# The recurrent stage of a two-block transformer kernel: unscaled sum transposed, projections scaled by a row on VectorE, low parts of the down-sized weights made by GpSimd

## What is computed

```python
h = _rmsnorm(x, g[1])                      # x * rsqrt(mean(x*x) + eps) * gain, by token
p = h @ w_in                               # 1024 -> 3*512 (convolution) + 1696 (recurrence)
gate_b, gate_c, h_in = jnp.split(p_conv, 3, axis=-1)
y_conv = gate_b * _short_conv(gate_c * h_in, conv_w)           # 3 taps over the tokens
p_rwkv = p_rwkv + (_shift(p_rwkv) - p_rwkv) * mu_shift         # mixed with the token before
r, k, v, dw, da, dg = jnp.split(p_rwkv, _RWKV_SPLITS, axis=-1)
# decay and iclr from dw and da, keys normalised by head, then for each token, 8 heads of 64:
#   S = S * w + (S a) b^T + v k^T ;  y = S r
# y normalised by head, plus a bonus term, times a gate
return jnp.concatenate([y_conv, y_rwkv], axis=-1) @ w_out
```

## Time and profile before

| | us |
|---|---|
| median of 3 runs | 1487.98 (1487.74 to 1488.11) |
| the profiled execution, its own time | 1488.31 |
| its span from first to last instruction | 1486.5 |
| TensorE busy in the span | 1471.3 (99%) |
| VectorE busy | 1005.7 (68%) |
| ScalarE busy | 853.0 (57%) |
| GpSimd busy | 507.2 (34%) |

### The profile page before, as it was taken

How to read it: one execution, slowest core, us unless ns; L and a number is a source line. 1 busy time by engine, 2 the same in 40 slices (tenths; PEclk the granted TensorE clock), 3 DMA queues, 4 the chain that set the end, 5 groups by cost and what they waited for, 6 DMA issues and landing times. The chain is left out here.

```text
span 1486.5 us, 25655 instructions
## 1 busy us (share of the span) xinstructions
PE 1471.3 (99%) x9545; PEld 1279.4 (86%) x9545; DVE 1005.7 (68%) x1304; ACT 853.0 (57%) x1316; POOL 507.2 (34%) x207
## 2 busy tenths in 40 slices
PE   9999999999999999999999999999999999999998
PEld 8888889888888888888988888888888887888886
DVE  6776567567777567765665776557765589877654
ACT  6555576445555565555675655555555678655544
POOL 2434400001444335444341444434344300144442
PEclk9999999999999999999999999999999999999999
DMA  7655542235565645555533565545655453265552
GB/s 260 226 206 197 184 142 86 89 115 184 198 199 186 208 157 186 207 191 192 184 115 114 187 206 190 193 156 191 209 195 186 170 202 110 100 213 186 206 184 87
DMA packets 48812, 259.99 MB, mean 175 GB/s; under 512 B 5584, under 2 KB 5968, under 8 KB 28144
## 3 DMA queue, kind: packets, MB, share of 16 engines
q1 hardware_dynamic: 29520, 190.49, 36.5%
q10 hardware_dynamic: 19152, 68.53, 14.0%
q0 software_dynamic: 80, 0.14, 0.0%
HBM read 258.08 MB, written 1.05 MB: 174 GB/s over the span
## 5 line engine op out<-in xcount | busy, mean ns | idle before, releaser
L379 POOL TENSOR_TENSOR dn_lo<-raw_dn,dn_hi 128x1024 fp32r<-128x1024 f32 x138 | 471.8, 3419 | 833.7 <-ACT dn_hi L362 824.8
L366 DVE TENSOR_TENSOR gu_lo<-raw_gu,gu_hi 128x2048 fp32r<-128x2048 f32 x161 | 369.4, 2294 | 182.7 <-ACT gu_hi L352 181.4
L612 PE MATMUL banks<-h_both,gu_hi 128*128 128x512 f32 x2016 | 478.2, 390 | 0.0
L612 PEld LDWEIGHTS banks<-h_both,gu_hi 128*128 128x128 f32 x2016 | 378.1, 188 | 78.4 <-ACT gu_hi L352 0.2
L352 ACT CAST gu_hi<-raw_gu 128x2048 fp32r<-128x2048 f32 x160 | 305.0, 1906 | 12.1 <-PE banks L386 12.0
L619 PEld LDWEIGHTS banks<-h_both,gu_lo 128*128 128x128 f32 x2016 | 258.5, 191 | 9.8
L619 PE MATMUL banks<-h_both,gu_lo 128*128 128x256 f32 x2016 | 261.6, 283 | 0.0
L386 PE MATMUL banks<-dn_hi,act_hi 128*128 128x512 f32 x528 | 207.2, 393 | 0.0
L386 PE MATMUL banks<-dn_lo,act_hi 128*128 128x512 f32 x528 | 207.2, 392 | 0.0
L386 PE MATMUL banks<-dn_hi,act_lo 128*128 128x512 f32 x528 | 205.6, 389 | 0.0
L559 DVE TENSOR_TENSOR silu<-silu,arena 128x256 f32<-128x256 f32 x126 | 179.1, 1421 | 4.3
(11 more groups left out here) (392 smaller groups left out, 1565.7 us busy)
## 6 DMA issues: line engine op xcount, KB each, us to landing
raw_gu<-units_gu SPq DMA_DIRECT2D x161, 1024.0 KB, 4.8
raw_dn<-units_dn ACTq DMA_DIRECT2D x130, 512.0 KB, 3.5
raw_dn<-units_dn SPq DMA_DIRECT2D x32, 512.0 KB, 3.5
...
```

Source lines behind the costliest of these rows:

```text
L366: nc.vector.tensor_tensor(gu_lo[:, p, :], raw_gu[:, p, :], gu_hi[:, p, :].bitcast(F32), ALU.subtract).then_inc(gu_lo_ready, 1)
L379: nc.gpsimd.tensor_tensor(dn_lo[:, p, 0:n], raw_dn[:, p, 0:n], dn_hi[:, p, 0:n].bitcast(F32), ALU.subtract).then_inc(dn_lo_ready, 1)
L612: ins = nc.tensor.matmul(banks[:, 2 * p + side, :], gu_hi[:, p, w], h_both[:, k, :, :].rearrange("p i t -> p (i t)"), start=k == 0, stop=F ...
```

## The change

It does three things in the even stage, and leaves the others alone:

- The start takes the feed-forward stages' way: `gained_pe` on TensorE, then squares and root on ScalarE behind `h_hi`, and a row of factors, which stands in `silu[:, 0, :]` (`even_row`). TensorE makes the row behind tile 2. The seven matmuls, the two scalings of `x` and the GpSimd steps for eps are gone.
- A new step `raw(i)` on VectorE multiplies each tile by the row as it reads it from PSUM: for mixed tiles into a buffer of four (`unmixed`), for tiles 14 to 25 right into their place. `evac(i)` and `mix(i)` then read that buffer in SBUF, and `evac` is gone for tiles 14 to 25. A tile's bank is free after `raw`.
- All twelve `dn_lo` of the stage are made by GpSimd (`lo_dn_pool`) and none by VectorE (`lo_dn`). GpSimd does them behind a memset that waits for both squares.

```diff
@@ -284,6 +284,7 @@
...
+        even_row = silu[:, 0, :]
...
@@ -478,21 +479,25 @@
...
+        def row_bank(s):
+
+            return 3 if stages[s] == "even" else 7
+
         def rstd_row_pe(pe, s):
...
-                ins = nc.tensor.matmul(banks[:, 7, t * P:(t + 1) * P], const("ones"), rstd_diag[:, t, :], start=True, stop=True)
+                ins = nc.tensor.matmul(banks[:, row_bank(s), t * P:(t + 1) * P], const("ones"), rstd_diag[:, t, :], start=True, stop=True)
...
-            nc.scalar.copy(rstd_row, banks[:, 7, 0:T]).then_inc(row_ready, 1)
+            nc.scalar.copy(even_row if stages[s] == "even" else rstd_row, banks[:, row_bank(s), 0:T]).then_inc(row_ready, 1)
...
-            return sum(k == "ffn" for k in stages[:s])
+            return sum(k in ("ffn", "even") for k in stages[:s])
...
@@ -876,30 +881,32 @@
...
-            dve = [("scaled", t, c) for t in range(2) for c in range(2)] + ["omu", "omka"] + mix(0, 5) + ["one_row", "key_ss"] + mix(5, 8) + ["kkn", "b", "at", "bt"]
-            dve += ["kh", "mt0", "mt1"] + mix(8, 9) + ["ab0", "ab", "kt"] + mix(9, 10)
+            raw = lambda *places: [("raw", i) for i in places]
...
+            dve += ["rb"] + raw(15, 16) + ["bv", "bv_b"] + raw(17) + ["uw"] + raw(18) + ["s1"] + conv(0) + raw(19)
+            dve += [("q", 0), ("q", 1)] + state(1) + raw(20) + [("y", 1)]
+            dve += conv(1) + state(2) + raw(21) + [("y", 2)] + conv(2) + raw(22) + [("y", 3)] + conv(3) + raw(23) + ["centred"]
+            dve += raw(24, 25) + [("y_conv", j) for j in range(3)] + [("conv_lo", j) for j in range(3)] + [("y_conv", 3), ("conv_lo", 3)]
...
-        x_ss, x_bias = mla_stats[:, 16:20], mla_stats[:, 20:22]
-        x_scaled = [arena[:, slot, 0:D] for slot in (RC, VC)]
...
@@ -969,6 +974,10 @@
...
+        def unmixed(i):
+
+            return c4(YC)[0:96 if i in LOW_TILES else P, i % 4, :]
+
...
@@ -977,12 +986,11 @@
...
-            for t in range(2):
-                after(pool, "act", ("square_x", t))
-                done(nc.gpsimd.tensor_scalar(x_bias[:, t:t + 1], x_ss[:, 2 * t:2 * t + 1], 1.0 / D, NORM_EPS, ALU.mult, ALU.add),
-                     ("bias_x", t))
             pool.wait_ge(squares_ready, 2 * s + 2)
             done(nc.gpsimd.memset(u_conv[:, :, 0:2], 0.0), "pads")
+            for u in range(11):
+                lo_dn_pool(pool, *unit(s, u))
+            lo_dn_pool(pool, *unit(s, 11), 64)
...
@@ -991,14 +999,10 @@
...
-                after(act, "pe", ("tile", i))
-                if i < MIXED:
-                    m = 96 if i in LOW_TILES else P
-                    ins = nc.scalar.activation(tile_target(i), tile_place(i), ACT.Copy,
-                                               scale=omu[0:m, mix_column(i):mix_column(i) + 1])
-                else:
-                    ins = cp(tile_target(i), tile_place(i))
-                done(ins, ("evac", i))
+                after(act, "dve", ("raw", i))
+                m = 96 if i in LOW_TILES else P
+                done(nc.scalar.activation(tile_target(i), unmixed(i), ACT.Copy,
+                                          scale=omu[0:m, mix_column(i):mix_column(i) + 1]), ("evac", i))
...
@@ -1022,30 +1026,12 @@
...
-            done(square_x(0, 0), ("square_x", 0))
-            square_x(0, 1).then_inc(squares_ready, 1)
-            done(square_x(1, 0), ("square_x", 1))
-            done(log_x(0), "ln_x0")
-            after(act, "act", "ln_x0")
-            done(nc.scalar.activation(rstd[:, 0:1], rstd[:, 0:1], ACT.Exp, scale=-0.5), "rstd_x0")
-            square_x(1, 1).then_inc(squares_ready, 1)
-            log_x(1).then_inc(rstd_ready, 1)
-            act.wait_ge(rstd_ready, rstds_before(s) + 1)
-            nc.scalar.activation(rstd[:, 1:2], rstd[:, 1:2], ACT.Exp, scale=-0.5).then_inc(rstd_ready, 1)
             h_hi_act(act, s)
-            nc.scalar.preload_act_table(ACT.Ln)
+            for t in range(2):
+                squares_act(act, s, t, loaded=True)
+            inverse_root_act(act, s)
             hi_gu(act, *unit(s, 1))
+            rstd_row_act(act, s)
             after(act, "dve", "omu")
             evac(0)
             evac(1)
...
-            evac(16)
...
-            evac(25)
...
@@ -1194,10 +1171,15 @@
...
+            def raw(i):
+                after(dve, "pe", ("tile", i))
+                place = tile_place(i)
+                done(tt(unmixed(i) if i < MIXED else tile_target(i), place, even_row[0:place.shape[0], :], ALU.mult), ("raw", i))
+
             def mix(i):
                 after(dve, "act", ("evac", i))
                 dst, m = tile_target(i), 96 if i in LOW_TILES else P
-                done(stt(out=dst[:, 1:T], in0=tile_place(i)[:, 0:T - 1], scalar=pcol("mu", mix_column(i), m), in1=dst[:, 1:T],
+                done(stt(out=dst[:, 1:T], in0=unmixed(i)[:, 0:T - 1], scalar=pcol("mu", mix_column(i), m), in1=dst[:, 1:T],
                          op0=ALU.mult, op1=ALU.add), ("mix", i))
 
...
@@ -1217,35 +1199,33 @@
...
-            dve.wait_ge(x_ready, 4 * s)
-            for t in range(2):
-                if t == 0:
-                    after(dve, "act", "rstd_x0")
-                else:
-                    dve.wait_ge(rstd_ready, rstds_before(s) + 2)
-                for c in range(2):
-                    done(ts(x_scaled[t][:, c * 512:(c + 1) * 512], quarter(t, c), rstd[:, t:t + 1], None, ALU.mult),
-                         ("scaled", t, c))
             done(ts(omu, cols("mu", 14), -1.0, 1.0, ALU.mult, ALU.add), "omu")
             done(ts(omka, cols("k_a", 4), -1.0, 1.0, ALU.mult, ALU.add), "omka")
             h_lo_dve(dve, s)
-            lo_dn(dve, *unit(s, 0))
+            rstd_row_dve(dve, s)
             lo_gu(dve, *unit(s, 1))
+            dve.wait_ge(row_ready, ffn_index(s) + 1)
+            raw(0)
+            raw(1)
             mix(0)
             mix(1)
-            lo_dn(dve, *unit(s, 1))
+            raw(2)
+            raw(3)
             mix(2)
             mix(3)
             lo_gu(dve, *unit(s, 2))
+            raw(4)
             mix(4)
             own(("mix", 4))
             nc.vector.memset(low(96, P, 0), 0.0)
             done(nc.vector.memset(low(DECAY_RANK, DECAY_RANK + 1, 0), 1.0), "one_row")
             after(dve, "pe", "key_norm")
             done(ts(split2(flat(INV)), two(6), 1e-24, None, ALU.max), "key_ss")
+            raw(5)
             mix(5)
-            lo_dn(dve, *unit(s, 2))
             lo_gu(dve, *unit(s, 3))
+            raw(6)
+            raw(7)
             mix(6)
             mix(7)
             after(dve, "act", "inv_k")
...
             done(tt(flat(KH), flat(KC), flat(AI), ALU.mult), "kh")
+            raw(8)
             after(dve, "pe", "ab")
             masked(MT, 2, "pairs2", "mt0")
             own("mt0")
@@ -1274,39 +1255,46 @@
             own("ab0")
             done(tt(prob(AB), prob(AB), const("eye2").rearrange("p (q t) -> p q t", q=1).to_broadcast([P, 16, CHUNK]), ALU.add),
                  "ab")
+            raw(9)
             done(tt(flat(KT_), flat(KH), flat(EM), ALU.mult), "kt")
             mix(9)
...
             level(3, ak)
-            level(4, lambda: lo_dn(dve, *unit(s, 5)))
+
+            level(4, lambda: raw(14))
...
+            raw(15)
             lo_gu(dve, *unit(s, 6))
+            raw(16)
...
-            lo_dn(dve, *unit(s, 6))
+            raw(17)
...
             def convolution(j):
                 u, y = u_conv[:, j, :], c4(CC)[:, j, :]
-                after(dve, "act", ("evac", 18 + j))
+                own(("raw", 18 + j))
...
+            raw(20)
             add_y(1)
...
             after(dve, "pe", "mean")
             done(stt(out=split2(flat(YS)), in0=two(2), scalar=-1.0 / 64, in1=split2(flat(YS)), op0=ALU.mult, op1=ALU.add),
                  "centred")
             lo_gu(dve, *unit(s, 9))
+            raw(24)
+            raw(25)
             for some in ((0, 1, 2), (3,)):
                 for j in some:
-                    after(dve, "act", ("evac", 22 + j))
                     own(("tap2", j))
+                    own(("raw", 22 + j))
                     done(tt(c4(YC)[:, j, :], c4(CB)[:, j, :], c4(CC)[:, j, :], ALU.mult), ("y_conv", j))
...
-            lo_dn(dve, *unit(s, 9))
...
@@ -1404,33 +1397,21 @@
...
             y_lo(3)
...
             lo_gu(dve, *unit(s, 11))
-            lo_dn(dve, *unit(s, 11), 64)
...
-            for i in range(7):
-                mm(banks[:, 3, :], h_hi[:, 0, 0:P], h_both[:, 0, :, :].rearrange("p i t -> p (i t)"), start=True, stop=True)
-            for t in range(2):
-                for b in range(4):
-                    if b % 2 == 0:
-                        after(pe, "dve", ("scaled", t, b // 2))
-                    for i in range(2):
-                        ins = nc.tensor.transpose(banks[:, b, i * T + t * P:i * T + (t + 1) * P],
-                                                  x_scaled[t][:, (2 * b + i) * P:(2 * b + i + 1) * P], ident)
-                    if t == 1:
```

(40 more changed lines are left out.)

36 lines of the change are left out of this document (9 added, 27 removed).

## The result

| | before | after |
|---|---|---|
| median of 4 runs, us | 1487.86 (1487.08 to 1488.11) | 1503.17 (1500.46 to 1504.54) |
| ratio | | 1.0103, 95% interval 1.009 to 1.0115 |
| the profiled execution's span | 1486.5 | 1502.7 |

The change costs 15.3 us, 1.0%. The forecast was 1499, range 1491.5 to 1503.5, so the median lies 0.3 us inside the range's upper end, and the profiled execution (1504.54) was the slowest of the four.

The account below looks back on a forecast made before the run. TensorE, busy 99% of the span, was taken to bound the kernel, with no slack behind its waits. Eleven places, from -2.90 at the seam to +3.1, summed to +10.9 us, about 1499; range 1491.5 to 1503.5.

Parts of the forecast that it names:

- Places 1 to 6 and 11: TensorE waits: seam -2.90, tile 2 +1.15, row +0.43, sum over heads +1.75, tanh +2.1, cumulative sums +3.1, first output row +2.1.
- Place 4: Sum over heads: TensorE waits for the last square of the keys on ScalarE, +1.75 us.
- 6: Cumulative sums: TensorE waits for iclr, as evac(6) waits for raw(6) behind gu_lo of unit 3, +3.1 us.
- 11: First row of the output: raw(25) stands ahead of y_conv on VectorE, +2.1 us.
- 5: Tanh: mix(4), both inputs now in SBUF, is held beside GpSimd's dn_lo of unit 2, +2.1 us.
- Places 8 and 9: turn_m, mt1 held by dn_lo of unit 3, +1.8 us; first joined blocks, behind raw(9), evac(9) and copies, +0.9.
- Place 7: Scores of the keys: b, at, bt follow mix(7), one raw later, +0.3 us (bounds 0 and 0.5).
- Place 10: Levels and states: idle time of ScalarE and VectorE covers nearly all, +0.15 us (bounds 0 and 1.0).
- the clock rival: TensorE's clock falls to 1.2 GHz after the wait at 6 or 11: +14 to +18 us, 1502 to 1506; chance 0.12.
- the seam of 4.97: TensorE's 4.97 us from the feed-forward stage's last product to the even stage's first; forecast to become 2.07.
- the seam less the row: Seam -2.90 plus row's matmuls +0.43, -2.5 us; alone, as the rival "only the seam counts", 1485.5, chance 0.08.

Follow-up runs that it names:

- e3: Changed kernel with raw(6) ahead of gu_lo of unit 3 on VectorE instead of behind it: 1496.8 us, ratio 1.0059.
- e4: Changed kernel with raw(25) behind the first three y_conv and conv_lo instead of ahead of them: 1498.1 us, ratio 1.0074.
- e5: Changed kernel with GpSimd's dn_lo of unit 2 waiting for mix(4) and that of unit 3 for ab: 1498.4 us, ratio 1.0068.
- e8: Changed kernel with raw(6) early, raw(25) late, GpSimd waiting for mix(4) and ab, dn_lo of unit 0 on VectorE, row ahead of tile 2: 1489.3 us.
- e11: Changed kernel with raw(25) late and 11 unread matmuls ahead of TensorE's wait for iclr: 1495.3 us, ratio 1.0054.
- e2: Kernel before with only all twelve dn_lo moved to GpSimd, start and mixing as before: 1491.5 us, ratio 1.0027.
- e9: e8's kernel with five more changes of order, each at a wait its profile still showed: 1487.7 us, ratio 1.0005 against the kernel before.

## Why the prediction held, and where not

- **Places 1 to 6 and 11** came within 0.25 us each, and each wait was named with its releaser. (Place 4 was put at 1.75 as the middle of 1.2 to 2.2 less the lag of a signal, which would be under 1.7; it measured 1.87.) e3, e4, e5 and e8 undid 6, 11, 5 and 4, and in their traces those steps went or fell (3.13 to 0.32, 2.01 to none, 1.92 to 0.77, 1.87 to 0.78). The times of the first three moved by more than the steps, since falls of the clock and the stops inside L1495 came or went with them.
- **Places 8 and 9** were right in sum (2.7) and depend on a race of 0.15 us, computed at the full clock. In the four traces with the sums at that clock they came as forecast, 1.8 and 0.9; in the profile after `mt1` was first. Who is first, `mt1` or `dn_lo`, decides only which of the two shows the wait. That "had `mt1` come first, it would cost 0" was wrong: the next instruction with two SBUF inputs, `mix(8)`, pays instead.
- **Place 7** was hidden in the profile after (behind the late start), and 0.35 in e3 for a forecast of 0.3. **Place 10** was mis-sized: 0.95 for 0.15 (bounds 0 and 1.0), mainly from a stop that the profile lays to nothing. Such stops differ from trace to trace: the same place made -0.5 in e3 and e4 and -1.9 in e11, so that part of any single sum is luck.
- **The step that failed is the weight of the clock rival.** The sum has no term for the clock, and so 1499 is 4.2 short of the median. That the median is inside the range is partly luck: it is so by 0.3 us, and only because the range took in half of that rival's case. I gave the rival 0.12, on the ground that the seam of 4.97 "left the clock full". In that seam TensorE was busy for all but 0.8 us, with the unread matmuls: it spoke of no idle time. A wait of 2.96 behind two of 1.7 was outside all that the trace had. The price that I gave, 3 to 7 us more, was right: 4.4 in the profile, and 4 to 5 between the 1498.5 and the medians of 1502.4 and 1503.2. The Trainium skill, "TensorE: Matmul & The Clock Gate", section "Why this matters for your kernels", warns of idle gaps between bursts of matmuls as throughput lost. The runs agree: all twelve falls stand at a wait of 1.85 to 2.96 us. e4 shows that a fall doesn't come each time.
- **That GpSimd holds VectorE** was right, and wider than I had it: instructions with one input, in SBUF, are held too (e2's large one, and the 128x2 `rstd_half`, 2.06 in the profile after for 0.16 before). The Trainium skill, "GPSIMD Engine Reference", section "Key points", names two-port modes of VectorE beside two SBUF inputs; I used the second half only. By the first half e2's `TENSOR_SCALAR` is held if it ran in such a mode; whether it did, no run here shows.
- **What the change is worth** is at most the seam less the row, 2.5 us; no order that I tried showed it in the time (e9: 0.7 over before, interval -0.6 to 2.1).
